# A two-block transformer on one core: the second block's mix projection and first up-projection chunks by token halves

## What is computed

```python
def second_block(x, ...):            # x: (1, 512, 1024), fp32
    a = rmsnorm(x, norm_pre_mix_2)
    mixed = token_mixer(a, ...)      # 4 mLSTM heads and 8 latent-attention heads, joined,
                                     # then @ w_out_2 (1024 x 1024): the "WO" projection
    h = x + rmsnorm(mixed, norm_post_mix_2)
    f = rmsnorm(h, norm_pre_mlp_2) @ w_up_2          # 1024 -> 4096: "up"
    y = square(relu(f)) @ w_down_2                   # 4096 -> 1024: "down"
    return h + rmsnorm(y, norm_post_mlp_2)

def rmsnorm(x, g):
    return x * rsqrt(mean(x * x, axis=-1) + EPS) * g
```

## Time and profile before

| | us |
|---|---|
| median of 3 runs | 1595.78 (1593.89 to 1597.19) |
| profiled execution: device time | 1594.33 |
| profiled execution: span in the trace | 1592.5 |
| mean granted TensorE clock, share of full | 0.992 |

### The profile page before, as it was taken

The page is one execution under the profiler, slowest core; times in us unless marked ns, Lnnn a source line. Parts: engine busy times, 40 slices in busy tenths (PEclk is TensorE's granted clock), DMA queues, the critical chain, the costliest instruction groups (busy, mean ns, idle before and its releaser), DMA issues.

```text
span 1592.5 us, 20823 instructions
## 1 busy us (share of the span) xinstructions
PE 1548.9 (97%) x7226; PEld 1277.3 (80%) x7226; DVE 834.7 (52%) x1455; ACT 649.5 (41%) x1045; POOL 665.7 (42%) x296
## 2 busy tenths in 40 slices
PE   7999999999999999999999999999998999999997
PEld 6888888777788877888888888877776788888887
DVE  5689999877785346442121134867645512121125
ACT  5553333444552445524233244555744423233231
POOL 4454444322344432444444445423525444444442
PEclk9999999999999999999999999999998999999999
DMA  5333323222333222332332332211112223333332
GB/s 201 93 124 101 93 94 104 66 67 66 107 98 101 92 66 67 101 104 93 95 103 92 94 104 94 83 58 60 41 54 66 93 93 105 94 92 102 95 93 80
DMA packets 41123, 144.56 MB, mean 91 GB/s; under 512 B 4564, under 2 KB 6740, under 8 KB 40792
## 3 DMA queue, kind: packets, MB, share of 16 engines
q1 hardware_dynamic: 40032, 139.94, 27.9%
q10 hardware_dynamic: 1016, 3.62, 0.7%
HBM read 141.43 MB, written 2.11 MB: 90 GB/s over the span
## 4 chain that ended last, share of the span: by engine, by line
PE 91%; DVE 3%; issue 3%; ACT 1%; POOL 1%; DMA 1%; SPq 0%; DVEq 0%; ACTq 0%; POOLq 0%
PE bank L474 90%; DMA w_raw<-in_stream 1%; PE bank L584 1%; POOL res L458 1%; DVE x_sq L1679 1%; PE bank L974 0%; POOL w_lo L393 0%; DVE bias L1752 0%; DVE xu_lo L1688 0%; ACT kT L1277 0%; ACT probs L1145 0%; DVE ffy L2372 0%; ACT w_hi L1112 0%; DVE q_ml L2223 0%; DVE bank L1646 0%
## 5 line engine op out<-in xcount | busy, mean ns | idle before, releaser
L393 POOL TENSOR_TENSOR w_lo<-w_raw,w_hi 128x1024 fp32r<-128x1024 f32 x256 | 618.0, 2414 | 863.6 <-ACT w_hi L1112 863.3
L1112 ACT CAST w_hi<-w_raw 128x1024 fp32r<-128x1024 f32 x256 | 268.6, 1049 | 502.0 <-DMA w_raw<-in_stream 501.9
L474 PE MATMUL bank<-a_hi,w_hi 128*128 128x512 f32 x1120 | 451.3, 403 | 6.6 <-DVE a_lo L1933 4.9
L474 PE MATMUL bank<-a_hi,w_lo 128*128 128x512 f32 x1120 | 438.0, 391 | 0.0
L474 PE MATMUL bank<-a_lo,w_hi 128*128 128x512 f32 x1120 | 437.7, 391 | 0.0
L474 PEld LDWEIGHTS bank<-a_hi,w_hi 128*128 128x128 f32 x1120 | 211.2, 189 | 55.8 <-issue 9.3
L474 PEld LDWEIGHTS bank<-a_lo,w_hi 128*128 128x128 f32 x1120 | 211.3, 189 | 48.0 <-issue 3.6
L474 PEld LDWEIGHTS bank<-a_hi,w_lo 128*128 128x128 f32 x1120 | 211.1, 188 | 44.5
L474 PE MATMUL bank<-b_hi,w_hi 128*128 128x512 f32 (+1 forms) x640 | 244.4, 382 | 0.0
L474 PE MATMUL bank<-b_hi,w_lo 128*128 128x512 f32 (+1 forms) x640 | 242.3, 379 | 0.0
L474 PE MATMUL bank<-b_lo,w_hi 128*128 128x512 f32 (+1 forms) x640 | 242.3, 379 | 0.0
(11 more groups left out here) (350 smaller groups left out, 1885.7 us busy)
## 6 DMA issues: line engine op xcount, KB each, us to landing
w_raw<-in_stream SPq DMA_DIRECT2D x256, 512.0 KB, 3.5
x_raw<-in_xT SPq DMA_DIRECT2D x4, 512.0 KB, 6.9
res<-in_xT ACTq DMA_DIRECT2D x1, 2048.0 KB, 7.5
out_y<-y_out SPq DMA_DIRECT2D x16, 128.0 KB, 1.8
mem_raw<-in_memT SPq DMA_DIRECT2D x1, 1024.0 KB, 12.1
mrow<-m_rows ACTq DMA_DIRECT2D x4, 256.0 KB, 3.2
consts<-in_consts SPq DMA_DIRECT2D x1, 452.0 KB, 10.2
posi<-in_positions ACTq DMA_DIRECT2D x1, 256.0 KB, 3.5
```

The source lines that it names most:

```text
L393: nc.gpsimd.tensor_tensor(w_lo[:, j, :], w_raw[:, j, :], w_hi[:, j, :].bitcast(F32), ALU.subtract).then_inc(w_lo_done, 1)
L474: return nc.tensor.matmul(o, l, r, start=start, stop=stop)
L1112: A.copy(w_hi[:, slot, :], w_raw[:, slot, :]).then_inc(w_hi_done, 1)
```

## The change

It has six parts.

1. **Mix rows out of `a_hi`.** `mix_hi`/`mix_lo` of k = 2, 3, 7 get places of their own, so that `a_hi`/`a_lo` can be written while WO is still running. The two waits that guarded the old places (for the chunk before WO) go.
2. **WO by halves.** Chunks 0 to 4 of WO stay whole. Chunks 5, 6, 7 are done for tokens 0 to 255 first (parts 0, 1, 2), then for 256 to 511 (parts 3, 4, 5). Sums, root, spreading and scales are done for each half: `wo_sums(0)` stands within part 3, `wo_scales(0)` within part 4; `wo_sums(1)` and `wo_scales(1)` stand after blocks 1 and 5 of the first half of the up chunks.
3. **Residual by halves.** Scaling, adding, rounding, squaring, remainder and the tree of squares run once for each half, with 128x256 operations, in an order written out by hand on VectorE, ScalarE and GpSimd. The tree of the first half stands ahead of the second half's scaling.
4. **Up chunks 0, 1, 2 by halves.** First halves of 0 and 1 block by block, first half of 2, then the second halves of all three block by block. The sum for the second norm stands after 6 of 8 blocks of chunk 3. ScalarE casts chunk 196 (up chunk 4) ahead of the root of the second norm.
5. **Two more banks.** Up chunks 4 and 5 of the first group write banks 6 and 7 and wait for no bank.
6. **In the attention units,** `pair_lo` stands ahead of `ml_first`, and the second series of taps starts at unit 4, not 5.

The diff, cut to its core:

```diff
+WO_WHOLE = 5
+WO_PARTS = [(j, h * HT, h * HT + HT) for h in range(2) for j in range(WO_WHOLE, KB)]
+WO_HALF = KB - WO_WHOLE
...
-CONV_AT = {0: 0, 5: 1}
+CONV_AT = {0: 0, 4: 1}
...
+                          (6, C0 + 30720, B0 + 10240), (1, G0 + 28800, B0 + 26624), (2, B0 + 6144, B0 + 8192),
+                          (3, BIAS0, BIAS0 + 2048), (7, BIAS0 + 4096, BIAS0 + 6144)):
...
+        def up_bank(s, g, o0, j):
+            if s == 1 and g == 0 and j in (4, 5):
+                return j + 2
+            return (o0 + j) % RING
...
-            for j in range(RING):
-                remainder(CH["FF2"] + j, j)
...
+            remainder(CH["FF2"], 0)
+            for j in range(1, 4):
+                post_add(0, j)
+            remainder(CH["FF2"] + 1, 1)
+            for j in range(4, KB):
+                post_add(0, j)
+            remainder(CH["FF2"] + 2, 2)
             for j in range(1, KB):
-                pool.wait_ge(sems["post_scaled"], j + 1)
-                pool.wait_ge(sems["x2_done"], KB)
-                nc.gpsimd.tensor_tensor(res[:, j, :], res[:, j, :], mixed[:, j, :], ALU.add
-                                        ).then_inc(sems["post_added"], 1)
+                post_add(1, j)
+            remainder(CH["FF2"] + 3, 3)
...
-            for j in range(KB):
+            for j in range(WO_WHOLE):
                 for i in range(6 if j < 2 else 0, KB):
                     wo_step(j, i)
-            token_scales((sems["ssq_added"], 4 * KB - 1), ssq, 2, last=((sems["res_sq"], 4 * KB), sq[:, (KB - 1) % 2, :]))
...
+            def wo_part(n, ks=range(KB)):
+                j, a, b = WO_PARTS[n]
+                c, o = CH["WO"] + j, O["WO"] + WO_WHOLE + n
+                if ks[0] == 0:
+                    if a == 0:
+                        pe.wait_ge(w_lo_done, c + 1)
+                    bank_free(o)
+                for k in ks:
+                    m = three(ps[o % RING][:, a:b], w_slot(w_hi, c % RING, k), w_slot(w_lo, c % RING, k),
+                              mix_hi[k][:, a:b], mix_lo[k][:, a:b], k == 0, k == KB - 1)
...
+            def wo_sums(h):
+                last = WO_HALF * (h + 1) - 1
+                pe.wait_ge(sems["part_ssq"], (WO_HALF - 1) * (h + 1))
+                pe.wait_ge(sems["part_sq"], last + 1)
+                for tb in range(2 * h, 2 * h + 2):
+                    b = slice(tb * P, (tb + 1) * P)
+                    mm(ps[STAT][:, tb:tb + 1], ssq[:, b], ones[:, 0:1], True, False)
+                    m = mm(ps[STAT][:, tb:tb + 1], sq[:, (WO_WHOLE + last) % 2, b], ones[:, 0:1], False, True)
+                m.then_inc(sems["half_sums"], 1)
+            def wo_scales(h):
+                pe.wait_ge(sems["spread_done"], 2 + h)
+                for tb in range(2 * h, 2 * h + 2):
+                    m = mm(ps[5][:, tb * P:(tb + 1) * P], ones, spread[:, tb, :])
+                m.then_inc(sems["scales_ready"], 1)
+            wo_part(0)
+            wo_part(1)
+            wo_part(2)
+            wo_part(3, range(5))
+            wo_sums(0)
+            wo_part(3, range(5, KB))
+            wo_part(4, range(3))
+            wo_scales(0)
+            wo_part(4, range(3, KB))
+            wo_part(5)
...
+            def up_half(j, h, k):
+                c, o = CH["FF2"] + j, O["FF2"] + j
+                t = slice(h * HT, h * HT + HT)
+                if h == 0 and k == 0:
+                    pe.wait_ge(w_lo_done, c + 1)
+                    bank_free(o)
+                pe.wait_ge(sems["hg_ready"], KB * (3 + h) + k + 1)
+                m = three(ps[o % RING][:, t], w_slot(w_hi, c % RING, k), w_slot(w_lo, c % RING, k),
+                          a_hi[:, k, t], a_lo[:, k, t], k == 0, k == KB - 1)
...
             def norm_pre_mlp():
-                pe.wait_ge(sems["post_tree"], 3)
+                pe.wait_ge(sems["post_tree"], 6)
                 mm(ps[STAT][:, :], ones, mixed[:, 0, :]).then_inc(sems["post_summed"], 1)
-            feed_forward("FF2", 1, 3, norm_pre_mlp, 3, upto=KB + WHOLE)
+            for k in range(KB):
+                up_half(0, 0, k)
+                up_half(1, 0, k)
+                if k == 1:
+                    wo_sums(1)
+                elif k == 5:
+                    wo_scales(1)
+            for k in range(KB):
+                up_half(2, 0, k)
+            for k in range(KB):
+                for j in range(3):
+                    up_half(j, 1, k)
+            feed_forward("FF2", 1, 3, norm_pre_mlp, 6, upto=KB + WHOLE, done=3)
...
                     A.activation(mcol[:, 3, :], mcol[:, 2, :], ACT.Sqrt).then_inc(sems["ml_root"], 1)
                 if st == 11:
                     act.wait_ge(sems["ml_gated"], h + 1)
-                    if h == 2:
-                        act.wait_ge(chunk_done, CH["WO"])
...
+            wo_square(0)
+            round_to(CH["FF2"] - AHEAD)
+            wo_square(1)
+            wo_square(2)
+            half_root(0, 1, STAT)
+            wo_square(3)
+            post_row(0, 0)
+            post_row(0, 1)
+            post_row(0, 2)
+            round_to(CH["FF2"] + 1 - AHEAD)
+            wo_square(4)
+            post_row(0, 3)
+            wo_square(5)
+            post_row(0, 4)
+            round_to(CH["FF2"] + 2 - AHEAD)
+            half_root(1, 2, STAT)
+            post_row(0, 5)
+            post_row(0, 6)
+            post_row(0, 7)
             round_to(CH["FF2"])
             for j in range(KB):
-                residual(4, 3, j, col("norm_pre_mlp_2", j), a_hi,
-                         (sems["post_added"], j) if j else (sems["post_first"], 1))
+                post_row(1, j)
+            round_to(CH["FF2"] + 1)
             root(9, rstd[:, :], STAT, 1.0 / D, sums=(sems["post_summed"], 1))
...
                 if n >= 8 and n % 8 == 2:
                     latent_scaled(n - 2)
-                ml_first(n)
                 if turning:
                     pair_lo(n // 8 - 1)
-                elif n >= 1:
+                ml_first(n)
+                if n >= 1 and not turning:
                     latent_scaled(n - 1)
...
-            for j in range(KB):
+            for j in range(WO_WHOLE):
...
+            def wo_out(n):
+                j, a, b = WO_PARTS[n]
+                if a == 0:
...
+            def post_scale(h, j):
+                t = slice(h * HT, h * HT + HT)
+                if j == 0:
+                    dve.wait_ge(sems["scales_ready"], 2 + h)
+                V.scalar_tensor_tensor(out=mixed[:, j, t], in0=mixed[:, j, t], scalar=col("norm_post_mix_2", j),
+                                       in1=ps[5][:, t], op0=ALU.mult, op1=ALU.mult).then_inc(sems["post_scaled"], 1)
                 if j == 0:
                     dve.wait_ge(sems["x2_done"], KB)
-                    dve.wait_ge(sems["post_scaled"], 1)
-                    V.tensor_tensor(res[:, 0, :], res[:, 0, :], mixed[:, 0, :], ALU.add).then_inc(sems["post_first"], 1)
-                if j >= 2:
-                    split_residual(3, j - 2, col("norm_pre_mlp_2", j - 2), a_hi, a_lo)
...
+            def post_split(h, j):
+                t = slice(h * HT, h * HT + HT)
+                dve.wait_ge(sems["hg_hi"], KB * (3 + h) + j + 1)
+                V.scalar_tensor_tensor(out=a_lo[:, j, t], in0=res[:, j, t], scalar=col("norm_pre_mlp_2", j),
+                                       in1=a_hi[:, j, t].bitcast(F32), op0=ALU.mult, op1=ALU.subtract
+                                       ).then_inc(sems["hg_ready"], 1)
+            def post_tree(h):
+                t = slice(h * HT, h * HT + HT)
+                dve.wait_ge(sems["post_sq"], KB * (h + 1))
+                for n, half in enumerate((4, 2, 1)):
+                    V.tensor_tensor(mixed[:, 0:half, t], mixed[:, 0:half, t], mixed[:, half:2 * half, t], ALU.add
+                                    ).then_inc(sems["post_tree"], 1)
+                    dve.wait_ge(sems["post_tree"], 3 * h + n + 1)
...
+            for n in range(WO_HALF):
+                wo_out(n)
+                if n < WO_HALF - 1:
+                    wo_add(n)
+            half_spread(0, 1)
+            wo_out(3)
+            wo_add(3)
+            post_scale(0, 0)
+            post_scale(0, 1)
+            post_scale(0, 2)
+            post_split(0, 0)
+            post_scale(0, 3)
+            post_split(0, 1)
+            wo_out(4)
+            post_split(0, 2)
+            wo_add(4)
+            post_scale(0, 4)
+            post_scale(0, 5)
+            post_split(0, 3)
+            post_scale(0, 6)
+            post_scale(0, 7)
+            wo_out(5)
+            post_split(0, 4)
+            post_split(0, 5)
+            half_spread(1, 2)
+            post_split(0, 6)
+            post_split(0, 7)
+            post_tree(0)
+            post_scale(1, 0)
+            post_scale(1, 1)
+            for j in range(2, KB):
+                post_scale(1, j)
+                post_split(1, j - 2)
+            post_split(1, KB - 2)
+            post_split(1, KB - 1)
+            post_tree(1)
```

(3 more changed lines are left out.)

145 lines of the change are left out of this document (85 added, 60 removed).

## The result

| | before | after |
|---|---|---|
| median, us | 1595.78 (7 runs, 1593.89 to 1597.19) | 1598.70 (7 runs, 1596.50 to 1601.07) |
| ratio to before, 95% interval | | 1.0021 (1.0012 to 1.0030) |
| span of the profiled execution | 1592.5 | 1596.4 |
| mean granted TensorE clock | 0.992 | 0.992 |

The change costs 2.9 us, 0.21%. The forecast was 1596.3 in 1590.5 to 1601.0, with "within 0.2%" as the likeliest case; the measured ratio lies on that bound, to the slow side.

A forecast was written before the change was run, and what follows sets the result against it. TensorE, busy 97% of the span, was taken as the bound through waits, clock and products. Pair turns -5.5 plus stage +6.0 gave +0.5: 1594.33 to 1594.8, plus 1.45 for a median of 1596.3, range 1590.5 to 1601.0.

The forecast's parts named there:

- pair turns: Attention part: earlier mix_lo gains 1.7 and a whole clock 2.8 at pair 0, 1.0 at pair 2; sum -5.5.
- the stage: WO to up: chunk 5 starts 3.0 later, lost clock adds 2.5 and 0.5; +6.0, bounds +1.0 to +8.5.
- So I take all 2.8 as gained: Pair 0: with about 1 of wait left, all 2.8 of slow clock work is won; bounds 0 and 2.8.
- Pair 2 as a proof that 2 us don't lose the clock: TensorE stood 2.14 at pair 2 with clock 1.00, so about 1 left at pair 0 should keep the clock.
- rival B: Pair 0: clock falls all the same, part one gives only 2.7; net +3.3, median 1599.1; chance 0.14.
- WO's end: WO ends at 1217.95, not 1215.7: 0.95 for half products at 0.120 and 1.34 for sums and scales.
- Waits 6.8 and slow clock 0.5: Up's half products: five TensorE waits of 2.4, 2.2, 1.4, 0.5 and 0.3, plus 0.5 of slow clock for short stops.
- rival C: WO to up: later cast 193, or clock already falling at 1218 to 1224, costs 8.5; net +3.0, median about 1599; chance 0.12.
- Held additions: Residual: VectorE's half additions take 2.41 beside GpSimd's remainder, 0.42 where nothing runs beside them.
- Rival A: Residual: VectorE is held less, norm's sum at 1243.1, chunk 5 at 1256.5; net -4.5, median 1591.3; chance 0.29.
- Chunk 5: Up chunk 5: weights 13.6 after the norm's sum, at 1261.0; TensorE waits 5 to 6, stage +3.0 before clock loss.
- After such a stop the clock falls, as it did after 4.89: Up chunk 5: half clock behind the new wait of 5 to 6 costs +2.5.

The follow-up runs named there:

- tuned_order: casts_behind_root with ScalarE's casts and second root, VectorE's copy of WO's last part and TensorE's blocks of chunk 192 reordered; median 1589.43 us, ratio 0.9958 to before.
- taps_only: The kernel before with only the second series of taps moved to unit 4, the pair's remainder left in place; median 1592.35 us, ratio 0.9985.
- casts_behind_root: The changed kernel, but ScalarE casts chunks 197 and 198 right behind the second norm's root; median 1591.06 us, ratio 0.9972 to before.
- split_products: tuned_order, but TensorE starts chunks 193 and 194 with products needing only w_hi, those with w_lo last; median 1588.67 us, ratio 0.9959 to before.
- halves_only: The changed kernel without part six (pair_lo and taps back in their old places); median 1602.49 us, ratio 1.0041 to before.
- pairs_only: The kernel before with part six alone (pair_lo ahead of ml_first, second taps at unit 4); median 1592.87 us, ratio 0.9982.
- norm_earlier: The changed kernel with the second norm's sum after 1 block of up chunk 3, chunk 196's cast behind the root; median 1593.18 us, ratio 0.9985 to before.
- sums_later: split_products with the sums of WO's second half after block 2 of the first up halves, not block 1; median 1587.14 us, ratio 0.9954 to before.

## Why the prediction came out as it did

The mechanism was right: a gain at the pair turns, and a greater loss because chunk 5's weights hang on the norm. The median came out 2.4 above the forecast: 2.2 from the pair turns, -0.4 from the stage, and 0.6 that the ruler of one execution each doesn't account for. A forecast net of +0.5 is less than what can be told here, so that its sign was right is in part luck.

- **Pair turns, -5.5 against -3.3.** Up to the first stop each step held: the wait left was 1.05 (about 1), the clock stayed at 1.00, the first product with `sT` moved as forecast, and by 1102.8 TensorE was 4.4 ahead (1.7 + 2.8 = 4.5 forecast). It kept 2.9 of it, and 0.3 of the 1.0 forecast at pair 2. The step that failed is "So I take all 2.8 as gained": the slow clock had been covering VectorE, which is now late with `o_rows` (0.82), and at pair 2 ScalarE is with `probsT` (0.59). tuned_order shows it from the other side, where the clock fell at pair 0 and cost about 0.15. The term for what is late next was missing from the sum. By the trace of taps_only the taps' move alone brings the 2.9 at pair 0; the remainder's new place adds nothing there.
- **Pair 2 as a proof that 2 us don't lose the clock.** It held for this execution, but taps_only shows the same stop with the clock lost, and casts_behind_root a stop of 1.05 at pair 1. Nor is "over some 2 us of standing in one stretch" what rival B decides from: tuned_order and split_products lost the clock at pair 0 behind 1.05. That the clock didn't fall in the changed kernel's trace is in part luck, and where it did fall it didn't cost the 2.8.
- **WO's end.** Forecast +2.26 against before; measured 1215.77 - 1215.69 on the axis of a kernel that is 2.2 ahead: +2.3. The half product's 0.120 held too wherever the clock was whole. The formula of the Trainium skill ("TensorE: Matmul & The Clock Gate", Back-to-back issue gap) for an isolated product gives an estimate of 0.109 for 256 columns; the trace differs by 0.011 and decides.
- **Waits 6.8 and slow clock 0.5.** Together 7.3; measured: the sum stands 30.7 behind WO's end, of which 22.7 is work, 3.5 is waits (2.37 as forecast, 1.13 in place of 2.2, none at row 5) and so some 4.5 slow clock: 8.0. The total was nearly right, its parts weren't: there are no stops at row 5 and beyond, where TensorE was itself slow. It is the mis-sized term of the stage: behind a stop of 2.4 among half products the clock is halved for nine us. This is what rival C was to be known by, the clock falling already at 1218 to 1224, but its price of 8.5 didn't come.
- **Held additions.** The forecast of 2.41 was met by 2.35, and 0.46 came where the remainder was cut short (forecast 0.42). The Trainium skill's "GPSIMD Engine Reference", 1. Specifications, says that VectorE's operations with two inputs in SBUF contend with GpSimd; this trace agrees, with 2.35 against 0.46. Rival A, in which VectorE is held less, is refuted: its sum at 1243.1 was to come 5.6 earlier than it did (1246.50, on the axis of a kernel that is 2.2 ahead).
- **Chunk 5.** Weights 13.6 behind the sum: 13.3. Wait 5 to 6: 4.87. Clock behind it 2.5: 1.6, by the ruler from +1.8 at chunk 5's start to +3.4. So chunk 5 started 4.0 later than it would have (forecast 3.0), and the clock cost 1.4 less than the 2.5 and 0.5 set aside for it: that the stage came within 0.4 of its forecast is two errors that nearly cancel. "After such a stop the clock falls, as it did after 4.89" also misreads the kernel before: its clock is 0.69 in 1220 to 1222, ahead of that stop, and 0.50 all through it. That the banks bring nothing while the cast stands behind the norm is worked out from rows, not run; that casts and banks are worth 7.6 together and the casts alone 2.0 is shown.
- **The frame.** I set the whole sum against one profiled execution. Its start lies 1.0 to 1.8 earlier than that of halves_only, pairs_only, norm_earlier and the changed kernel. That may be most of the 1.45 between its time and the median, but no trace of an execution at the median was kept to show it. A comparison of two spans would have been wrong by 1.1 at the start and 0.5 at the end.

What stays open: why the clock falls behind one stop and not behind another of the same length, in the same program; and what the banks bring without the casts, which was not run.

## What to carry to other kernels

Ask of each added resource (here two banks) what else its user waits for, and move that in the same edit: a one-line change in ScalarE's order made the difference between 2.9 slower and 4.8 faster. When a chain of engines is drawn later by finer work in front of it, list everything that hangs on its end, weights included, not only the data. And when a stop or a slow clock is removed, put a term into the sum for the engine that the stop was hiding. One trace in which the clock held is no proof that it holds; look at the same place in every trace that has the same program there.

## What the runs showed of the hardware

- A stop of the same length at the same place (2.14 at pair 2) left the granted clock at 1.00 in one kernel's execution and at 0.79 in another's. Behind a stop of 1.05 at pair 1 it was 1.00 in the changed kernel and 0.66 over five us in casts_behind_root, whose program is the same up to there; that cost 1.6. Behind stops of 0.98 and 0.35 in sums_later it was 0.54 and 0.60 over eight us. The length of one stop does not decide it.
- A GpSimd subtraction of 128x1024 holds a 128x256 VectorE operation with both inputs in SBUF until it ends (2.35, 2.67; 0.46 where it was cut to one block). VectorE's copies of 128x512 out of PSUM take the same 0.68 to 0.69 beside such a subtraction and alone; the earlier trace rows has one beside it.
- The first 60 us of a kernel differ by up to 2.3 between profiled executions (the thirteenth cast at 65.87 to 68.19) with the same program there. The late ones are those in which the clock was halved for a part of 30 to 36 (0.66 in 30 to 35 in the changed kernel, 1.00 in the kernel before). Differences of under 2 us between spans have to be read behind that point.
